# Prompt attention in another order of pairs, reciprocals spread by transposes, and parts of the pooling mixer moved

## What is computed

```python
y = concat([oa, ob]) @ w_out          # oa: 8 heads of 64, window of 128 keys, a learned sink per head, 2 kv heads
                                      # ob: 8 heads of 64, branches (window, dilation) (128,1) (512,4) (2048,16)
xp = xp + _rms(mp, gl[1])             # mp: attention (layer 0) or pooling mixer (layer 1)
xp = xp + _rms(_sq_relu_mlp(_rms(xp, gl[2]), mlp_w1[l], mlp_w2[l]), gl[3])
# pooling mixer: per channel group of 256 the trailing mean over 2/4/8/16 rows minus the row itself,
z = jnp.einsum('ntgc,gce->ntge', y, w_pool).reshape(n, t, D_MODEL)
return z * pool_scale
```

## Time and profile before

| | |
|---|---|
| median of 3 runs | 2305.12 us (2304.23 to 2306.57) |
| profiled execution | 2304.14 us |
| its span (first to last instruction) | 2302.3 us |
| mean granted clock of PE | 0.993 |
| prompt attention | 260.7 to 455.4 us |
| pooling mixer and start of the second MLP | about 1465 to 1540 us |

### The profile page before, as it was taken

The page is one execution under the profiler, slowest core; times in us unless marked ns, Lnnn a source line. Parts: engine busy times, 40 slices in busy tenths (PEclk is TensorE's granted clock), DMA queues, the critical chain, the costliest instruction groups (busy, mean ns, idle before and its releaser), DMA issues.

```text
span 2302.3 us, 34288 instructions
## 1 busy us (share of the span) xinstructions
PE 2236.2 (97%) x14129; PEld 2011.3 (87%) x14129; DVE 950.5 (41%) x1671; ACT 669.1 (29%) x1311; POOL 136.9 (6%) x202
## 2 busy tenths in 40 slices
PE   6999999998999999999999999989999999999998
PEld 6999877777789899898998997889989899898996
DVE  4210265566544334243342336573424334243346
ACT  4211486545333113021130223342203112031121
POOL 1000121000120000000000003230000000000001
PEclk9999999999999999999999999999999999999999
DMA  5221400099422112021020222221202112021123
GB/s 166 77 77 40 156 2 1 12 384 352 133 84 74 43 31 66 7 73 50 23 73 0 73 82 91 85 102 49 64 10 73 32 41 64 9 73 36 36 85 121
DMA packets 125778, 175.68 MB, mean 76 GB/s; under 512 B 14509, under 2 KB 94437, under 8 KB 125548
## 3 DMA queue, kind: packets, MB, share of 16 engines
q1 hardware_dynamic: 121500, 169.53, 22.4%
q10 hardware_dynamic: 4176, 4.72, 0.6%
HBM read 155.88 MB, written 18.58 MB: 76 GB/s over the span
## 4 chain that ended last, share of the span: by engine, by line
PE 75%; DVE 2%; DMA 1%; issue 1%; ACT 0%; SPq 0%; POOL 0%; DVEq 0%; POOLq 0%; ACTq 0%
PE ps L1701 32%; PE ps L1681 32%; PE ps L2535 4%; PE ps L2488 1%; DMA sa_va<-cache_a_v 1%; PE ps L1360 1%; PE ps L1690 1%; PE ps L1417 1%; PE ps L2505 1%; PE ps L1380 0%; DVE t_xn L1474 0%; DVE m_xT_lo L2304 0%; DVE t_zn L1474 0%; PE ps L2555 0%; SPq L655 0%
## 5 line engine op out<-in xcount | busy, mean ns | idle before, releaser
L1645 DVE TENSOR_TENSOR t_y<-t_y,ps 128x512 f32<-128x512 f32 x288 | 197.7, 687 | 627.3 <-PE ps L1701 627.2
L1701 PE MATMUL ps<-t_w_hi,t_h_hi 128*128 128x512 f32 x1152 | 450.3, 391 | 5.0 <-DVE t_y L1645 2.8
L1701 PE MATMUL ps<-t_w_lo,t_h_hi 128*128 128x512 f32 x1152 | 448.9, 390 | 0.0
L1701 PE MATMUL ps<-t_w_hi,t_h_lo 128*128 128x512 f32 x1024 | 399.1, 390 | 0.0
L1681 PE MATMUL ps<-m_xT_lo,t_w_hi 128*128 128x384 f32 x1488 | 328.0, 328 | 0.0
L1681 PE MATMUL ps<-m_xT_hi,t_w_lo 128*128 128x384 f32 x1488 | 328.0, 328 | 0.0
L1681 PE MATMUL ps<-m_xT_hi,t_w_hi 128*128 128x384 f32 x1488 | 327.9, 328 | 0.0
L1576 ACT ACTIVATE t_relu<-ps 128x384 f32<-128x384 f32 (+1 forms) x192 | 87.9, 458 | 809.8 <-PE ps L1701 776.7
L1606 DVE TENSOR_TENSOR t_w_lo<-t_raw,t_w_hi 128x1024 fp32r<-128x1024 f32 x128 | 155.4, 1224 | 276.7 <-ACT t_w_hi L1564 276.4
L1701 PEld LDWEIGHTS ps<-t_w_hi,t_h_hi 128*128 128x128 f32 x1152 | 216.7, 188 | 53.1 <-DVE t_y L1645 4.1
L1681 PEld LDWEIGHTS ps<-m_xT_hi,t_w_hi 128*128 128x128 f32 x1488 | 254.8, 188 | 1.1
(11 more groups left out here) (214 smaller groups left out, 2572.5 us busy)
## 6 DMA issues: line engine op xcount, KB each, us to landing
t_raw<-mlp_w SPq DMA_DIRECT2D x128, 512.0 KB, 4.0
sa_kb<-cache_b_k SPq DMA_DIRECT2D x40, 512.0 KB, 8.5
sa_vb_even<-cache_b_v SPq DMA_DIRECT2D x20, 512.0 KB, 12.1
sa_vb_odd<-cache_b_v SPq DMA_DIRECT2D x20, 512.0 KB, 11.2
in_raw<-attn_w_in SPq DMA_DIRECT2D x6, 1024.0 KB, 6.0
t_rows<-scratch_x SPq DMA_DIRECT2D x12, 512.0 KB, 5.7
qT<-x_prompt SPq DMA_DIRECT2D x8, 512.0 KB, 3.7
t_rows<-x_prompt SPq DMA_DIRECT2D x8, 512.0 KB, 3.5
```

The costliest lines, as they stand in the source:

```text
L1645: self.nc.vector.tensor_tensor(part, part, self.core.ps[:, 6 + n % 2, :], ALU.add).then_inc(self.part_added, 1)
L1701: mm = self.nc.tensor.matmul(self.core.ps[:, 6 + half, :], a[:, k, t * P:t * P + P], w[:, k, half * 512:(half + 1) * 512], start=(k == 0 a ...
```

## The change

It has three parts. **Order:** the pairs are no longer taken row by row. All A pairs of rows 1 to 7 are put, two at a time, behind the B pairs of rows 0 to 3, and the B pairs of rows 4 to 7 follow without a break. The closings move with them, query pieces are made for two pairs at a time, and DVE takes every odd group of transposes, of A too. **Reciprocals:** DVE computes each reciprocal for all 64 columns of its head (128x512) and four transposes turn the result. **Mixer:** the scaling of the pool weights goes from POOL to DVE; the mixes of tiles 0 to 2 go into the last down block, with a gain buffer, a transfer and work buffers of their own; turns take turns in two sets of banks; the orders on PE, ACT, DVE and POOL follow.

```diff
+    sequence = [(0, j) for j in range(4)]
+    windows = [(i, j) for i in range(1, PT) for j in range(4)]
+    for i in range(PT):
+        for j in range(4, KT):
+            sequence.append((i, j))
+            for _ in range(2):
+                if windows:
+                    sequence.append(windows.pop(0))
+    place = {pair: p for p, pair in enumerate(sequence)}
+    closing = [2 * p + 1 for p, (_, j) in enumerate(sequence) if j % 4 == 3]
...
-        if wide(u):
-            return u
-        return u - 1 if u >= 2 and wide(u - 2) else u - 2
-
-
-    copier = [int(n % 2 == 1 and u % HEADS >= NH and k > 0) for n, (u, _, k) in enumerate(groups)]
+        return u if wide(u) else u - 2
+
+
+    copier = [int(n % 2 == 1 and k > 0) for n, (u, _, k) in enumerate(groups)]
...
-            if 1 <= step <= U and step % NH == 0:
-                i, d = divmod(step - NH, HEADS)
-                dve.wait_ge(exped, step)
-                nc.vector.reciprocal(rden[:, i, d:d + NH], den[:, i, d:d + NH]).then_inc(rden_ready, 1)
...
+            if step - 2 in closing:
+                x = rounds[step - 2]
+                i, j, _ = parts_of(step - 2)
+                d = 2 * j + 2 - NH
+                dve.wait_ge(exped, step - 1)
+                if x >= 1:
+                    dve.wait_ge(turned, spread_index[x - 1] + 1)
+                nc.vector.reciprocal(rden[:].rearrange("p (h d) -> p h d", h=NH),
+                                     den[:, i, d:d + NH].rearrange("p (h o) -> p h o", o=1).to_broadcast([P, NH, HD])
+                                     ).then_inc(rden_ready, 1)
...
                 for p in range(4):
-                    for half in range(2):
-                        d = 2 * (j - 3 + p) + half
-                        last = nc.tensor.matmul(core.ps[half * HD:(half + 1) * HD, 4 + n % 2, p * P:(p + 1) * P],
-                                                rden[:, i, d:d + 1].to_broadcast([P, HD]), core.identity[:],
-                                                start=True, stop=True)
+                    last = nc.tensor.transpose(core.ps[:, 4 + n % 2, p * P:(p + 1) * P], rden[:, p * P:(p + 1) * P],
+                                               core.identity[:])
...
-            post0.root(core, pool, 0)
-            pool.wait_ge(weights_in, 16)
-            pool.wait_ge(scale_in, 16)
-            scale_weights(0)
-            scale_weights(1)
-            for q in (1, 2):
+            for q in range(3):
                 post0.root(core, pool, q)
...
             def finish0(n):
-                if n == 3:
+                if n in (1, 2):
+                    scale_weights(n - 1)
+                elif n == 3:
                     m0.take_sample(dve)
...
+                    if n // 2 in (6, 7, 8):
+                        add_z(n // 2 - 6)
...
                 for q in {4: (0,), 5: (1, 2), 6: (3,), 7: (4,), 8: (5,)}.get(p, ()):
                     pooling(q)
+                if 5 <= p < 5 + EARLY_Z:
+                    mix(p - 5)
...
-            mix(0)
             pooling(6)
-            mix(1)
+            mix(3)
             pooling(7)
-            mix(2)
+            mix(4)
             pooling(8)
-            mix(3)
+            mix(5)
             pe.wait_ge(yT_ready, NT)
-            mix(4)
-            for q in range(5, NT):
-                turn(q - 5)
-                mix(q)
+            turn(0)
+            turn(1)
+            mix(6)
+            turn(2)
+            mix(7)
+            turn(3)
+            mix(8)
             turn(4)
             turn(5)
```

More of the change, by code:

```diff
@@ L758, in is_spread @@
         return groups[n][2] == 0
+    spread_index = [n for n in range(len(groups)) if is_spread(n)]
     def before(n):
@@ L781, in batches_at @@
                 if step_of[min(n + 1, len(groups) - 1)] == step]
+    taken_at = {}
+    for u in closing:
+        following = (of_pair[u - 1][-1] // 2 + 1) * 2
+        taken_at.setdefault(step_of[min(following + 1, len(groups) - 1)] if following < len(groups) else STEPS, []).append(u)
     def turned_after(u):
@@ L823, in wait_for_copy @@
             nc.tensor.wait_ge(copied[copier[n]], mine.count(copier[n]))
-    def split_pieces(step):
[L828 to L833, removed]
+    pieces = []
+    for i in range(PT):
+        first_used = min(place[i, 0], place[i, 4])
+        pieces.append((max(-1, first_used - 5), i, None))
+        for j in range(0, KT, 2):
+            free = place[i - 1, j + 1] + 1 if i > 0 else -1
+            pieces.append((max(free, place[i, j] - 4), i, j))
+    pieces.sort(key=lambda piece: piece[0])
+    piece_no = {(i, j): n for n, (_, i, j) in enumerate(pieces)}
+    assert all(p < (place[i, j] if j is not None else place[i, 0]) for p, i, j in pieces)
+    LEADING = 3
+    assert [j for _, _, j in pieces[:LEADING]] == [None, 0, 2]
+    def split_pieces(step):
+        return [n for n, (p, _, _) in enumerate(pieces) if n >= LEADING and max(p, 0) * 2 + 1 == step]
     def piece_views(n):
-        i, kind = divmod(n, 3)
+        _, i, j = pieces[n]
         c = slice(i * P, (i + 1) * P)
-        if kind == 0:
+        if j is None:
             return [(kaT[:, c], k_hi[:, 0, c], k_lo[:, 0, c]), (kbT[:, :, c], k_hi[:, 1:, c], k_lo[:, 1:, c])]
-        pairs = slice(4 * (kind - 1), 4 * kind)
+        pairs = slice(j, j + 2)
         return [(qT[:, pairs, c], q_hi[:, pairs, :], q_lo[:, pairs, c])]
@@ L847, in lo_pieces @@
     def lo_pieces(n):
-        return sum(1 + (m % 3 == 0) for m in range(n))
+        return sum(1 + (j is None) for _, _, j in pieces[:n])
     def wait_for_scores(eng, n):
-        i, kind = divmod(n, 3)
-        if kind > 0 and i > 0:
-            eng.wait_ge(scored, HEADS * (i - 1) + NH * kind)
+        _, i, j = pieces[n]
+        if j is not None and i > 0:
+            eng.wait_ge(scored, 2 * place[i - 1, j + 1] + 2)
     def sync(sp):
@@ L868, in gpsimd @@
     def gpsimd(pool):
[L869 to L875, removed]
+        for n in range(len(pieces)):
+            pool.wait_ge(hi_done, lo_pieces(n + 1))
+            for x, (src, hi, lo) in enumerate(piece_views(n)):
+                if lo_pieces(n) + x > 0:
+                    pool.wait_ge(lo_done, lo_pieces(n) + x)
+                nc.gpsimd.tensor_tensor(lo, src, hi.bitcast(F32), ALU.subtract).then_inc(lo_done, 1)
         pool.wait_ge(turned, len(groups))
@@ L884, in leading_parts @@
     def leading_parts():
-        high_piece(0)
-        high_piece(1)
+        for n in range(LEADING):
+            high_piece(n)
     def scalar(act):
@@ L2073, in _ @@
             pre_pool.root(core, pool, NT - 1)
-            for q in range(NT):
+            for q in range(EARLY_Z):
+                pre1.root(core, pool, q)
+            for q in range(EARLY_Z, NT):
                 post_pool.root(core, pool, q)
-                if q >= 1:
+                if q > EARLY_Z:
                     pre1.root(core, pool, q - 1)
```

146 lines of the change are left out of this document (91 added, 55 removed).

## The result

The changed kernel takes 2326.75 us (median of four, 2320.6 to 2329.5) against 2305.85: a ratio of 1.0091, 95% interval 1.0079 to 1.0103. It is 21 us slower, where 2294 was forecast, and lies above the forecast's range of 2279 to 2314.

The account below looks back on a forecast made before the run. PE was taken to bound the kernel, with DVE becoming the bound of attention's first part. From 2305.1 us, attention -4 and mixer -7 gave 2294, with an overall range of 2279 to 2314.

Parts of the forecast that it names:

- the first part: First 48 pairs of prompt attention: DVE's work sums to 103 us, PE's to 90; 104 us taken.
- Second part: Last 16 wide pairs of prompt attention: PE's work 80 us, with waits 87.
- the push of the next biases: In the 16 wide pairs: three reciprocals push the next biases back 3 us each, some 2 covered; 3 us lost.
- The reciprocal: On DVE, sixteen times in attention: grows from 128x8 to 128x512 and takes 2.97 us each.
- the row with 148 ns as the fixed part: Alternative price of the wide reciprocal: one-element copy as fixed part, 6.4 ns per element, 3.4 us.
- The spread: On PE in attention: four transposes replace eight products, sixteen times -0.43, so -7 us of PE.
- The order: In attention: row starts and their clock falls gone, some 10 us of PE gained, mostly eaten by DVE.
- The mixer: Around the last down block: scaling on DVE gives -3.6 us; with the early mixes -7 in all.
- the early mixes: Three mixes moved ahead of the last down block's end save PE idle time; with the scaling, -7 us.
- (b): Rival: reciprocal dearer still, gain eaten from 3.7 us each; at 4.4 us the kernel takes 2316. Chance 0.20.
- (a): Rival: reciprocal runs like a copy, 0.69 us; attention 177 us, kernel 2280. Chance 0.16.
- (c): Rival: gaps at the reciprocals lower PE's clock, twelve falls cost 10 us; 2304, no change. Chance 0.14.

Follow-up runs that it names:

- E9: Changed kernel with 128x8 reciprocals and eight products, plus an idle 128x512 reciprocal on DVE behind each, read by nobody: 2328.5 us, ratio 1.0104.
- E10: Changed kernel with 128x8 reciprocals and eight products, plus an idle 128x256 reciprocal on DVE behind each: 2298.9 us, ratio 0.9968.
- E6: Changed kernel with 128x8 reciprocals, spread over 128x512 by a copy on DVE, four transposes kept: 2289.6 us, ratio 0.9915.
- E1: Changed kernel with reciprocals as before (128x8, spread by eight products), all else of the change kept: 2293.1 us, ratio 0.9946.
- E8: Kernel before with only the scaling of pool weights moved from POOL to DVE: 2301.6 us, ratio 0.9979.
- E3: Kernel before with the mixer's part of the change alone: 2304.6 us, ratio 0.9997.
- E13: Kernel before with the whole mixer part, and on PE mix 3 ahead of pooling 6: 2300.6 us, ratio 0.9977.
- E5: Changed kernel with each 128x512 reciprocal cut into four of 128x128, spread over later steps: 2327.6 us, ratio 1.0094.
- E7: Changed kernel with 128x8 reciprocals, spread over 128x512 by a copy on POOL, transposes kept: 2291.8 us, ratio 0.9940.

## Why the prediction was wrong

**The step that failed** is "DVE becomes the bound of this part ...; with what is lost at the hand-overs I take 104". It treated the first part as a sum of DVE's work plus a microsecond for all the waits, and left no half clock in it. The sum came out (103, measured 100.1), in part by luck: the reciprocals took 36.8 us where it had 34.8, with one fewer in this part, and the rest 63.3 where it had 68.0. The time was 119.6. A sum bounds a time from below; here the three engines work in order, PE's scores lead the biases by two units only, and what keeps DVE longer than that lead hides goes through ACT to PE. E9 and E10 measure it: of 1.70 us more at each closing the kernel loses 0.4, of 3.30 us it loses 2.2. Half clock is part of that: PE was busy 96.1 us in this part, where the sum had 90 and the same work takes 83.6 with cheap reciprocals (E6).

**Second part**, forecast 87, measured 97.0 with wide and 88.0 with cheap reciprocals [E6]. The term for the push of the next biases by "three reciprocals", 3 us, was too small for the same reason: there are five in this part, and they cost 9.0. Without that term the sum was 84 against the 88.0 of E6, where PE is busy 84.4 us (the sum had 80) and idle 3.6 (it had 4).

**The reciprocal**: 2.97 taken, 3.34 measured. That is 16 x 0.37 = 6 us more of DVE's time, a small part of the miss; the row with 148 ns as the fixed part gave the better estimate. The Trainium skill ("VectorE: DVE Perf Modes", section "🔬 Walkthrough: the 8-slice pipeline in each mode") led to an estimate of 4.3 us by eight cycles an element. The row differs: 6.24 ns are 6.0 cycles at the 0.96 GHz of that page's "Specifications", and the measurement decides.

**The spread**: forecast -7 us of PE; its busy time in attention is 6.0 us less in E6 than in E1 (168.0 and 174.0), and attention got 4.0 of it.

**The order**: right in kind. E1's attention is 13 us shorter with the old reciprocals, where some 10 were forecast, and scores wait for biases 0.8 us in all, where they waited 9.7.

**The mixer**: the scaling's -3.6 was right (-4.2 in E8). The other half, the early mixes, to -7 in all, was wrong: my walk missed that pooling 6 loses the mix that covered its input, and 4 us were given back as a wait and a fall of the clock (E3, E13). With that mended the early mixes still gained nothing, since PE waits as long at the turns as it did at the end.

**The rivals.** (b) had the right side by the wrong price: it needed 3.7 us for no gain, and 3.34 us lost 21. Its slope, a microsecond per microsecond, was about right on average: from E6 to the changed kernel DVE does 16 x (3.34 - 0.67) = 43 us more (0.20 for the small reciprocal and 0.475 for the copy), and attention takes 39 longer. But E9 and E10 show that the line is not straight, nearly free up to 1.7 us and steeper behind it. (a) forecast 177 us of attention for a reciprocal as cheap as a copy; E6, which has that price, took 177.5. (c) was at work: it had 10 us for the falls, and from E6 to the changed kernel PE's work takes 14.8 us longer. What it lacked is the 24 us of waits beside them. Its premise, that the clock falls behind waits of over 1 us, held only in part: in the changed kernel the clock was 0.50 in 363 to 366, behind a wait of 2.12 us, and 1.00 in 319 to 322, behind one of 2.70. It was given 0.14.

**What stays open**: behind attention the profiled executions take 1842 (E9) to 1852 us (E6) in kernels that are the same there. I leave that as the scatter of single executions, but it is not small beside the differences of 2 to 5 us that are read from one trace here. Whether a long hold of DVE costs more than the same time in pieces is open too (E5).

## What to carry to other kernels

Before work is moved to an engine because it is idle half the time, ask how far the engine that feeds on it can run ahead. In this pipeline, with a lead of two units, only a part of the added work was free (some 1.1 to 1.3 us at each closing), and cutting it into pieces that come later only moved the waits to the one who needs the result. An operation whose cost grows per element is done on the few distinct values, and spread by a copy. And a piece of PE work that looks movable may be the cover of the next piece's input.

## What the runs showed of the hardware

DVE's reciprocal costs about 6.2 ns an element: 199 ns for 128x8, 944 for 128x128 (E5), 1702 for 128x256 (E10), 3302 (E9) and 3343 for 128x512. A copy of 128x512 takes 475 ns (E6, both sides in SBUF) or 687 (out of PSUM), and 610 on POOL (E7). Taking the reciprocal's input with a step of zero over 64 columns adds nothing that shows: the 8 elements of the small one, each read once, fit the same line.

PE's clock fell to 1.2 GHz behind a wait of 1.29 us (E3, 0.50 in 1482 to 1485) and behind one of 2.12 (changed kernel, 0.50 in 363 to 366), but not behind waits of 1.38 us (E6, 1.00 in 382 to 385) and 2.70 us (changed kernel, 1.00 in 319 to 322). The length of the last wait alone does not say whether it falls.
